# A mixture-of-experts kernel: the second layer of each expert is placed before the last block of the next expert's first layer

## The reference

```python
logits = (hf @ router_w + router_b)
top_val, top_idx = lax.top_k(logits, TOP_K)          # 4 of 32 experts for each of 512 tokens
gate = softmax(top_val)
# for every expert e, over the rows (tokens) that chose it:
u = hf[toks] @ w1[e] + b1[e]                          # first layer: 1024 -> 2048
g_, lin = u[:, :1024], u[:, 1024:]
g_ = minimum(g_, 7.0);  lin = clip(lin, -7.0, 7.0)
y = ((lin + 1.0) * g_ * sigmoid(1.702 * g_)) @ w2[e] + b2[e]   # second layer: 1024 -> 1024
out[tok] += y * gate
```

## Time and profile before

| | us |
|---|---|
| median of 3 runs | 1884.92 |
| lowest, highest | 1881.42, 1884.98 |
| the profiled execution | 1886.29 |
| its span (first to last instruction) | 1884.2 |
| busy: TensorE, VectorE, ScalarE, GpSimd | 1780.1, 689.2, 388.3, 139.2 |

### The profile page before, as it was taken

The page is one execution under the profiler, slowest core; times in us unless marked ns, Lnnn a source line. Parts: engine busy times, 40 slices in busy tenths (PEclk is TensorE's granted clock), DMA queues, the critical chain, the costliest instruction groups (busy, mean ns, idle before and its releaser), DMA issues.

```text
span 1884.2 us, 31809 instructions
## 1 busy us (share of the span) xinstructions
PE 1780.1 (94%) x13076; PEld 829.1 (44%) x13076; DVE 689.2 (37%) x1751; ACT 388.3 (21%) x908; POOL 139.2 (7%) x209
## 2 busy tenths in 40 slices
PE   5999999899999999999999989999989889999998
PEld 3567657446333333333333323333333365666854
DVE  3469775613223222232322313122222243386140
ACT  2127521602111111111101101011111021271110
POOL 2020000000011011001111101011010100000000
PEclk9999999997999999999999989999999999999999
DMA  9912224132999999999999999999999892100001
GB/s 323 299 46 91 90 95 163 61 112 93 341 390 399 399 405 398 407 393 401 399 400 402 402 391 401 402 401 379 410 394 410 319 331 71 45 1 1 1 1 45
DMA packets 133402, 495.23 MB, mean 263 GB/s; under 512 B 22587, under 2 KB 72677, under 8 KB 84104
## 3 DMA queue, kind: packets, MB, share of 16 engines
q1 hardware_dynamic: 116624, 466.91, 63.8%
q0 software_dynamic: 11264, 19.27, 4.3%
q10 hardware_dynamic: 5368, 7.00, 1.0%
HBM read 481.08 MB, written 17.43 MB: 265 GB/s over the span
## 4 chain that ended last, share of the span: by engine, by line
PE 67%; DMA 20%; DVE 7%; issue 2%; SPq 1%; ACT 1%; POOL 0%; ACTq 0%; DVEq 0%; POOLq 0%
PE bank L1702 22%; DMA ring<-in_exp_w_dram 18%; PE bank L1725 10%; PE bank L434 10%; PE bank L447 8%; PE bank L974 6%; DVE arena L722 2%; DVE arena L691 1%; PE bank L1690 1%; PE bank L409 1%; SPq L1097 1%; DMA arena<-in_x_dram 1%; DVE arena L904 1%; PE bank L1675 1%; PE bank L1891 1%
## 5 line engine op out<-in xcount | busy, mean ns | idle before, releaser
L1702 PE MATMUL bank<-ring,arena 128*32 128x512 f32 x5568 | 641.3, 601 | 30.1 <-DMA ring<-in_exp_w_dram 20.8
L1702 PEld LDWEIGHTS bank<-ring,arena 128*32 128x32 f32 x5568 | 171.5, 110 | 383.0 <-issue 332.3
L1725 PE MATMUL bank<-ring,arena 128*32 128x512 f32 (+1 forms) x3392 | 307.6, 516 | 14.2 <-DMA ring<-in_exp_w_dram 12.8
L1725 PEld LDWEIGHTS bank<-ring,arena 128*32 128x32 f32 x3392 | 109.3, 110 | 215.3 <-issue 171.1
L434 PE MATMUL bank<-hT,ring 128*128 128x512 f32 x448 | 201.2, 602 | 2.1 <-ACT hT L962 1.1
L1404 ACT ACTIVATE arena<-bank,mod,small 128x96 f32<-128x96 f32 (+2 forms) x256 | 87.6, 424 | 552.2 <-PE bank L1690 552.2
L2174 DVE COPY arena<-bank 128x8 f32<-128x8 f32 (+1 forms) x32 | 5.3, 165 | 369.0 <-PE bank L1675 359.0
L434 PEld LDWEIGHTS bank<-hT,ring 128*128 128x128 f32 x448 | 85.3, 193 | 105.0 <-issue 102.2
L447 PE MATMUL bank<-ring,hT 128*128 128x256 f32 (+1 forms) x640 | 127.2, 359 | 0.0
L2188 DVE TENSOR_TENSOR arena<-bank,arena 128x512 f32<-128x512 f32 x87 | 54.9, 684 | 188.4 <-PE bank L1702 188.4
L447 PEld LDWEIGHTS bank<-ring,hT 128*128 128x128 f32 x640 | 111.8, 190 | 17.0 <-issue 3.3
(11 more groups left out here) (417 smaller groups left out, 1578.4 us busy)
## 6 DMA issues: line engine op xcount, KB each, us to landing
ring<-in_exp_w_dram SPq DMA_DIRECT2D x384, 1024.0 KB, 26.8
ring<-in_ada_w_dram SPq DMA_DIRECT2D x24, 1024.0 KB, 11.7
ring<-in_w_in_dram SPq DMA_DIRECT2D x23, 1024.0 KB, 11.9
ring<-in_w_out_dram SPq DMA_DIRECT2D x8, 1024.0 KB, 5.1
arena<-in_x_dram ACTq DMA_DIRECT2D x1, 2048.0 KB, 17.0
ring<-in_w_in_dram SPq DMA_DIRECT2D x8, 256.0 KB, 5.0
expert_sums<-arena POOLq DMA_DIRECT2D x4, 512.0 KB, 4.2
h_rows<-arena ACTq DMA_DIRECT2D x4, 512.0 KB, 2.6
```

What stands on the lines that cost most here:

```text
L1702: mm = pe.matmul(bank[g][QUAD * c:QUAD * (c + 1), :].rearrange("p (h n) -> p h n", h=2), rowsT[:, k, QUAD * g:QUAD * (g + 1)], w[:, :, SW ...
L1725: mm = pe.matmul(bank[b][QUAD * c:QUAD * (c + 1), 0:width], rowsT[:, g, 2 * q + j, :], w[:, col:col + width], start=(q == 0 and j == 0), s ...
```

## The change

TensorE does the second layer of expert n-1 not after block 7 of expert n's first layer but between its blocks 6 and 7 (`place_before`, called from `between` at k = 6). The waits for `dst`, `meta` and `at_ok` move with it. At n = 32, where there is no first layer, it stands alone as before. SyncE asks for the weights in the same order: seven first-layer blocks of expert n, the four second-layer blocks of n-1, then block 7. ScalarE does `rows_done` of an expert before the sigmoid (`gates_of`) of the next, which follows the order of TensorE. No instruction is added or removed.

```diff
+        SECOND_AFTER = 6
@@ SyncE
                 for k in range(8):
+                    if n >= 2 and k == SECOND_AFTER + 1:
+                        second_rows_of(e_last, n - 1)
                     sp.wait_ge(w1_used, 8 * (n - 1) + k + 1)
                     first_rows(e, k, landed[k])
-                if n >= 2:
-                    second_rows_of(e_last, n - 1)
                 e_last = e
@@ ScalarE
+                if 1 <= n < NEXP:
+                    if n >= 2:
+                        act.wait_ge(main.free, n - 1)
+                    rows_done(main, n, meta_r[(n - 1) % 4], QUADS[n - 1])
                 if n < NEXP:
                     gates_of(main, n + 1, QUADS[n])
-                if n >= 1:
-                    if n < NEXP:
-                        if n >= 2:
-                            act.wait_ge(main.free, n - 1)
-                        rows_done(main, n, meta_r[(n - 1) % 4], QUADS[n - 1])
@@ TensorE
+                    if k == SECOND_AFTER and n >= 1:
+                        place_before()
+
+                def place_before():
+                    if n + 1 < NEXP:
+                        pe.wait_ge(main.dst, n + 2)
+                    if n + 2 < NEXP:
+                        pe.wait_ge(main.meta, n + 3)
+                    pe.wait_ge(main.at_ok, n)
+                    second_layer(main, actT, QUADS[n - 1], wait_slot, True)
@@
-                if n >= 1:
-                    if n + 1 < NEXP:
-                        pe.wait_ge(main.dst, n + 2)
-                    if n + 2 < NEXP:
-                        pe.wait_ge(main.meta, n + 3)
-                    pe.wait_ge(main.at_ok, n)
-                    second_layer(main, actT, QUADS[n - 1], wait_slot, True)
+                if n == NEXP:
+                    place_before()
```

## The result

The changed kernel takes 1923.16 us (median of 4 runs, 1919.39 to 1924.82) against 1884.91 us: a ratio of 1.0211, 95% interval 1.0196 to 1.0226. It is slower by 38.3 us. The profiled execution took 1924.36 us, its span is 1922.4.

What follows compares the result with a forecast made beforehand. The weight stream was the bound, TensorE some 4% behind. TensorE's work 955.5, less block 7's 1.8, plus stalls 60.7, remaining falls 3.4 and new falls 31 gave 1048.8 against 1008.9 us, +39.9: 1924.8 us, range 1890 to 1960.

Steps and rivals of the forecast that it cites:

- The copy-out: Start of experts 2 to 31: TensorE waits for VectorE's bias adds out of the banks, 60.7 us of new stalls.
- The reserve: Expert 1's first layer to expert 30's second: TensorE needs 962.2 of 1008.9 us, leaving 46.7 us of waits.
- Falls of the clock: After new stalls of 2.06 us or more TensorE's clock halves: 14 falls at 2.2 us, 31 us.
- TensorE's own work: Expert 1's first layer to expert 30's second: layers, b2 products and the branch gap sum to 955.5 us.
- The moved waits: Waits for dst and meta after block 6 have 3.7 us of cover, at_ok enough time too: nought.
- the requests: SyncE's weight requests follow the order of use and the queue keeps the same distance: nought.
- the order on ScalarE: rows_done ahead of gates_of: its two copies are short, so the sigmoid isn't late: nought.
- The tail: After expert 30's second layer: the last second layer waits 4.9 us, but an 18.3 us chain keeps the length: 0.
- The first: Rival: the stalls come at the expert starts but the clock holds, +8.9 us, 1893.8 us; chance 0.20.
- The third: Rival: weights stay the bound, stalls and falls stay under 46.7 us of waits, 1882 us (faster form 1878); chance 0.07.
- The second: Rival: nearly every stall brings a long fall of the clock, 76 us, +85 us in all, 1970 us; chance 0.08.
- the fourth: Rival: moved waits for dst and meta bite, each us over the 3.7 us cover costing 30 us; chance 0.03.

Runs made afterwards that it cites:

- the fillers: Changed kernel plus one or two 512-column TensorE products of no use ahead of each wait for u_in, with 128 rows each: 1899.67 us, ratio 1.0091.

## Why the prediction was right, point by point

- **The copy-out.** 60.7 us of new stops were worked out from one adjacency in the trace of before; 60.5 us were measured, with 2.06, 1.46, 2.65 and, behind b2 products, 2.68 and 2.09 us for single ones.
- **The reserve.** 46.7 us of waits that new work must fill first; 49.4 us by the run with half the bytes, one fall of the clock included. No wait for weights is left, and halving the bytes of the changed kernel changes nothing: TensorE bounds the whole stretch.
- **Falls of the clock.** 14 were assumed at 2.2 us, 31 us. There were 13 at 1.9 us, 24.6 us by the slow blocks and 23.5 by the fillers. That the count came so close is partly luck. The rate, three in five of all stops of 2.06 us or more, was a good mean for the wrong reason: it is 4 of 13 for the plain stops of 2.06 us and 7 of 7 from 2.65 us up. And other profiles with the same stops have 8 to 14 falls. The two falls that stay cost 3.0 us instead of 3.4, the branch's gap 4.7 instead of 5.5.
- **TensorE's own work.** This term was too small. The stretch of 1048.5 us less 65.2 of stops and gap and 27.6 of falls leaves 955.7 us, where 955.5 - 5.5 - 1.8 = 948.2 had been put. Some 5 of the 7.5 us are one effect: undisturbed groups overlap by 0.18 us (515.64 + 10.50 is 0.18 past 525.96), more than the few hundredths that were named ahead of the prediction. So a time from start to start leaves the last product's end out; where a stop follows, that end is bare, an estimated 29 x 0.18 = 5.2 us. The other 2.3 us were not traced. That the sum came out at 1048.8 against 1048.5 us is luck: the falls were over-sized by 6.8, the branch's gap by 0.8 and the stops by 0.2, and this term was under-sized by 7.5.
- **The moved waits, the requests, the order on ScalarE.** Nought, as said, as far as the time shows; the runs show the price of the first two where their cover is taken away, 32 us and 11 us. The cover of 3.7 us for dst and meta was read rightly.
- **The tail.** The last second layer stops for 5.2 us (4.9 worked out) and takes 8.66 instead of 7.05 us with a fall, and the waiting for the sums is gone; before, a fall slowed the L1833 products that follow (9.64 us). From the end of expert 30's second layer to the end of those products it is 27.7 us against 27.9. Nought, as said, but by two things that cancel: the chain worked out at 18.3 us takes 20.3 (1539.5 to 1559.8), with a fall that wasn't foreseen, and the L1833 products behind it take 7.41 instead of 9.64.
- **The rivals.** The first, stalls without falls, was built by the fillers: 1899.7 us against 1893.8 worked out; the bare ends, some 5 us, are most of the difference. The third, the weights as the bound, needed copy-outs under 1.5 us; with 0.9 us stops, and 1.53 behind b2 products, the time is indeed that of the kernel before. The second and the fourth didn't come: 13 of 29 stops fell, and no wait for dst or meta appeared.

## What to carry to other kernels

Two resources that are level in a profile leave a reserve that can be counted, here 47 us of 1009. New work on the engine behind, spread over the stage, was free up to that and cost in full past it, so sum it before an order is changed. When steps of an in-order engine change places, ask of each pair that becomes adjacent whether the second writes what a third engine must still read from the first; one block of other work between them, or a signal for each bank, took the whole cost away. Ask for weights in the order of use, and price a regular stop with the clock as well as with its length.

## What the runs showed of the hardware that was not expected

- TensorE's clock fell after stops of 1.53 us when a product of 32 rows stood before them (7 of 8), and not after plain stops of 1.46 us (none of 24 in four profiles) or 0.9 us.
- The same stops don't bring the same falls each time: 13, 14, 10 and 8 falls behind the same 29 stops in four profiles. At 2.06 us the clock fell after 15 of 52, at 2.65 to 2.69 us after 25 of 28.
- In the stops behind b2 products fillers of 128 rows prevented every fall; fillers of 32 rows and nearly the same length left seven of eight, with 0.2 us more idle time. The two times differ by 13 us.
